# Cutting each weight remainder on GpSimd in four pieces: a two-block fp32 transformer kernel

## The reference

```
for l in range(2):                       # block 1
    h = rms_norm(x, norm_mix_pre[l])
    m = hybrid_mixer(h, w_in[l], ...)    # differential + dilated attention, gates
    x = x + rms_norm(m, norm_mix_post[l])
    h = rms_norm(x, norm_ffn_pre[l])
    g, u = split(h @ w_gate_up[l])       # hidden size 2816
    x = x + rms_norm((silu(g) * u) @ w_down[l], norm_ffn_post[l])
```

## Time and profile before

| | |
|---|---|
| median of three runs | 3269.81 us |
| profiled execution | 3269.45 us |
| its span, first to last instruction | 3267.7 us |
| mean granted TensorE clock | 0.996 of full speed |
| TensorE busy | 3184.0 us (97%) |
| VectorE busy | 1642.2 us (50%) |
| ScalarE busy | 1342.5 us (41%) |
| GpSimd busy | 1378.8 us (42%), 1175.1 of it in L437 |
| DMA | 335.40 MB, mean 103 GB/s |

### The profile page before, as it was taken

How to read it: one execution, slowest core, us unless ns; L and a number is a source line. 1 busy time by engine, 2 the same in 40 slices (tenths; PEclk the granted TensorE clock), 3 DMA queues, 4 the chain that set the end, 5 groups by cost and what they waited for, 6 DMA issues and landing times. The chain is left out here.

```text
span 3267.7 us, 45371 instructions
## 1 busy us (share of the span) xinstructions
PE 3184.0 (97%) x15969; PEld 2535.7 (78%) x15969; DVE 1642.2 (50%) x2602; ACT 1342.5 (41%) x2106; POOL 1378.8 (42%) x696
## 2 busy tenths in 40 slices
PE   8999999999999999999999999999999999999998
PEld 6778887788887778887788886777888867778887
DVE  6853337655627853337655534853333248533332
ACT  6765554322226765553322224454222245532222
POOL 3233334544454223334544454544444535444444
PEclk9999999999999999999999999999999999999999
DMA  3122222255522122222255523202222231122232
GB/s 140 58 81 87 82 86 78 103 188 197 188 102 80 61 78 88 87 87 77 101 201 184 191 94 107 78 31 80 96 96 97 99 116 65 40 84 96 96 103 103
DMA packets 94314, 335.40 MB, mean 103 GB/s; under 512 B 11072, under 2 KB 12288, under 8 KB 93952
## 3 DMA queue, kind: packets, MB, share of 16 engines
q1 hardware_dynamic: 92480, 327.65, 28.9%
q10 hardware_dynamic: 1728, 6.36, 0.5%
HBM read 331.83 MB, written 8.44 MB: 104 GB/s over the span
## 5 line engine op out<-in xcount | busy, mean ns | idle before, releaser
L437 POOL TENSOR_TENSOR wLo<-wring,wHi 128x1024 fp32r<-128x1024 f32 x482 | 1175.1, 2438 | 1709.8 <-ACT wHi L417 1709.4
L461 PE MATMUL psG<-hHi,wHi 128*128 128x512 f32 x2992 | 1185.3, 396 | 12.5 <-DVE ra L1296 4.3
L461 PE MATMUL psG<-hLo,wHi 128*128 128x512 f32 x2992 | 1170.5, 391 | 8.3 <-POOL hLo L486 7.2
L461 PE MATMUL psG<-hHi,wLo 128*128 128x512 f32 x2992 | 1166.0, 390 | 0.0
L417 ACT ACTIVATE wHi<-wring 128x1024 fp32r<-128x1024 f32 x482 | 510.3, 1059 | 970.6 <-PE psG L461 924.0
L461 PEld LDWEIGHTS psG<-hHi,wHi 128*128 128x128 f32 x2992 | 562.6, 188 | 153.6 <-issue 33.1
L461 PEld LDWEIGHTS psG<-hLo,wHi 128*128 128x128 f32 x2992 | 561.8, 188 | 140.1 <-POOL hLo L486 22.1
L461 PEld LDWEIGHTS psG<-hHi,wLo 128*128 128x128 f32 x2992 | 563.0, 188 | 112.9 <-issue 0.5
L461 PE MATMUL psG<-hidHi,wHi 128*128 128x512 f32 x704 | 274.0, 389 | 1.0 <-DVE branch L1453 1.0
L461 PE MATMUL psG<-hidLo,wHi 128*128 128x512 f32 x704 | 273.9, 389 | 0.0
L461 PE MATMUL psG<-hidHi,wLo 128*128 128x512 f32 x704 | 273.9, 389 | 0.0
(11 more groups left out here) (320 smaller groups left out, 3380.0 us busy)
## 6 DMA issues: line engine op xcount, KB each, us to landing
wring<-in_w SPq DMA_DIRECT2D x494, 512.0 KB, 3.2
modw<-in_wmod SPq DMA_DIRECT2D x96, 512.0 KB, 5.4
e_copies<-e_rows ACTq DMA_DIRECT2D x8, 512.0 KB
T_tab<-e_copies SPq DMA_DIRECT2D x4, 1024.0 KB, 5.5
mask<-in_mask SPq DMA_DIRECT2D x2, 1536.0 KB, 5.9
xin_sb<-in_x SPq DMA_DIRECT2D x4, 512.0 KB, 5.1
e_copies<-e_rows ACTq DMA_DIRECT2D x8, 256.0 KB
out<-o_sb SPq DMA_DIRECT2D x4, 512.0 KB, 3.8
```

What stands on the lines that cost most here:

```text
L437: pool.tensor_tensor(wLo[:, c % CUTS, :, :], wring[:, c % RING, :, :], wHi[:, c % CUTS, :, :], ALU.subtract).then_inc(w_cut[c % CUTS], 1)
L461: mm = pe.matmul(psG[:, G.slot(u), :], w[:, c % CUTS, k, :], r(j), start=start and j == 0 and n == 0, stop=stop and j == len(kts) - 1 and ...
```

## The change

Each call of cut_rest issues four subtractions of two channel tiles (256 columns) each in place of one of eight channel tiles (1024 columns). The semaphore is raised once, by the fourth.

```diff
@@ -58,6 +58,7 @@
 CUTS = 2
 MODS = 6 * DM // P
 MW = 1536 + 2 * P
+PIECE = KT // 4
@@ -434,7 +435,10 @@
         def cut_rest(pool, c, i=None):
 
             until(pool, w_high, c + 1 if i is None else i * RING + (c + 1))
-            pool.tensor_tensor(wLo[:, c % CUTS, :, :], wring[:, c % RING, :, :], wHi[:, c % CUTS, :, :], ALU.subtract).then_inc(w_cut[c % CUTS], 1)
+            for k in range(0, KT, PIECE):
+                ins = pool.tensor_tensor(wLo[:, c % CUTS, k:k + PIECE, :], wring[:, c % RING, k:k + PIECE, :], wHi[:, c % CUTS, k:k + PIECE, :],
+                                         ALU.subtract)
+            ins.then_inc(w_cut[c % CUTS], 1)
```

## The result

The changed kernel takes 3340.78 us (median of four runs, 3339.24 to 3342.39) against 3269.87 us for the kernel before, measured beside it. The ratio is 1.0217, with a 95% interval of 1.0205 to 1.0229: 70.9 us slower. The profiled execution took 3342.39 us, its span is 3340.6, 72.9 more than before.

A forecast was written before the change was run, and what follows sets the result against it. TensorE, busy 3184.0 of 3267.7 us, bounds the kernel, so added waits count at once. Terms 63 + 9.5 + 3 + 5.6 - 3 + 0.8 = 79 us on 3269.8 gave 3349, range 3280 to 3362.

The forecast's parts named there:

- all turns taken: Block 1's gate-up: VectorE takes three turns between the pieces of one chunk, 2.84 us more; chance 0.62, range 3325 to 3362.
- the rival that keeps VectorE out: GpSimd runs its four pieces without letting VectorE in; only 0.41 us per chunk counts, 3282 or about 3275; chance 0.17.
- The fixed part: Every GpSimd cut: four pieces take 2.80 us against 2.39 for one instruction, 0.41 more per chunk; bounds zero and 0.53.
- The price of a turn: VectorE getting in between two pieces costs GpSimd 0.45 us for 512 columns, 0.99 for 1024; bounds zero, 0.54 and 1.08.
- Block 1's gate-up: Three VectorE turns in one chunk add 2.84 us against room of 1.36 or 1.44; 44 tiles at 1.44, 63 us.
- The short chunks: Down projections: 28 chunks following a short one have room 0.07 us, each 0.34 over, 9.5 us.
- the leftover products: Four modw products per layer left over at the start of the down projection: 3 us.
- The attention stages: Rope tiles of the first attention and at the second's start: 5.6 us lost in two layers, 3 taken back.
- The room of GpSimd's chunk: Usable slack from GpSimd's end to the chunk's first weight load: 1.36 us in block 1's gate-up, 0.95 next chunk.
- The rival of one product alone: Block 1's gate-up: the second product misses its boundary, a tile costs 0.45 us; 36 us in all, 3306; chance 0.13.
- the faster rival: VectorE's earlier results outweigh GpSimd's later ones: at most 7.8 us of TensorE's waits come back, 3262; chance 0.03.

## Why the prediction was right

The forecast was 3349 us with a range of 3280 to 3362; measured were 3340.8. The forecast's own range, with all turns taken, was 3325 to 3362 and holds it too; the wider one reached down to 3280 only for the rival that keeps VectorE out. The mechanism with its place held: VectorE takes three turns between the four pieces in block 1's gate-up, and the run with the delayed products shows that the turns cost the stretch its time. That the sum of 79 came so near the 70.9 is in part luck: the gate-up was 3 us too dear, the down projections 4 and the branch products 4, and the attention stages 5 too cheap.

*The fixed part.* Taken as 0.41 us per chunk, from back-to-back pairs; an undisturbed cut takes 2.82 us against 2.39, so 0.43. The bound of 0.53, from reported durations, was too high, and the advice to go by the spacing of starts (the Trainium skill, Perfetto Trace Analysis, GPSIMD Engine Instruction) agrees with the trace: a piece reports 0.74 us and starts 0.69 after the last.

*The price of a turn.* Taken as 0.45 and 0.99; the pieces show 0.45 and 0.98. The 0.09 that a turn is cheaper than what VectorE still needs was right.

*Block 1's gate-up.* Taken as 44 x 1.44 = 63 us. Two tiles of the same kind start at 663.31 and 687.85, so two chunks take 12.27 us against 10.88: 1.39. The stretches hold 57.1 us and the last tile of each layer, in the down projection, about 2.8. The 0.05 to 0.09 less have a reason in the rows: after a late chunk the second weight load follows the first after 0.11 us and not 0.23.

*The short chunks.* Taken as 28 x 0.34 = 9.5, with 3 for the leftover products. The four down projections lose 11.1 us, of which 2.8 belong to the gate-up's last tiles, so 8.3. The 3 us for the leftover products do not show in the net: in layer 2 the chunk after the first short one starts 1.0 us later than the pieces alone make it, and in layer 1 the kernel before had itself lost 1.4 us at 887.70, where the load waits for VectorE's copy (L1453), of which 1.0 is gone. Of a wait like that one the prediction said nothing, and a single layer can carry it or not. Here too the first 0.34 is partly given back: after 905.76 the next chunk starts 5.35 us later and not 5.44. In these rows the remainder ends at 905.71 and the load follows at once, as in the earlier trace rows with no room left:

```profile
902.89 2.82 POOL L439 TENSOR_TENSOR wLo<-wring,wHi 128x256 fp32r<-128x256 f32 x4 [2.98 <-ACT wHi L418]
...
905.76 0.19 PEld L465 LDWEIGHTS psG<-hidHi,wHi 128*128 128x128 f32 x1 [0.40 <-POOL wLo L439]
```

*The attention stages.* This term failed in size and in its make-up. I had +5.6 for chunks without room and -3 for VectorE's earlier results, 2.6 in all; the two stages give +7.4. The first attention is a gain (-1.7 in sum: each layer loses 1.7 in its first rope tiles and wins 2.6 after them). The second loses 9.1, or 4.5 a layer. Part of that is the first rope tile there (1.2 a layer, where I had 0.86). Another part is a step that I did not have: VectorE's rotation product (L1295, now L1299) used to start just when GpSimd's cut ended, and now meets the last piece. VectorE, then GpSimd:

```profile
265.35 1.00 DVE L1299 TENSOR_TENSOR tmp<-tmp,ropes 128x512 f32<-128x512 f32 x1 [16.98 <-ACT tmp L1007]
```

```profile
262.98 2.82 POOL L439 TENSOR_TENSOR wLo<-wring,wHi 128x256 fp32r<-128x256 f32 x4 [3.54 <-ACT wHi L418]
```

The cut ends at 265.80; the product needs 1.00 us instead of 0.69, and the instruction behind it (L1300), which frees the PSUM buffer, comes so much later; the chunks of the rope tiles start 0.1 to 0.3 us late. That the one causes the other was read from the trace and not tried. The group's mean went from 692 to 879 ns. The room of GpSimd's chunk says nothing of this: it is a wait in the other direction. The last part, 1.6 us a layer, is TensorE's clock, for which the prediction had no term. After the first rope tile TensorE waits 2.25 us for the remainder, until the load at 196.74, and from 198.0 to 201.4 the granted clock is 0.5 of full speed, the lower of its two levels (1.2 GHz): weight loads start 0.43 us apart there and not 0.23. The same stretch of the changed kernel, and of the run with block 1's gate-up in one piece, whose load comes at 194.26 after the same wait (columns as in the earlier trace rows; the clock is the third number from the end):

```profile
198.00:202.00 4.00, 4.00 (x12) 3.15 (x11) 2.39 (x3) 0.47 (x1) 1.91 (x3) 0.58 0.60 205
```

```profile
195.50:199.50 4.00, 4.00 (x19) 3.27 (x18) 2.38 (x3) 0.50 (x1) 1.94 (x3) 1.00 0.62 201
```

Five runs have the four pieces and the wait of 2.25 us at this place, each in two layers. In five of these ten layers the clock falls behind the wait (both of the changed kernel, layer 2 of the run just named), and in these the second attention takes 353.5 us, in the other five 351.7 to 352.0. In the kernel before, where the wait is 1.01 us, it falls in neither layer. So 3.3 of the 9.1 us are the clock's; what decides whether it falls after a given wait stays open.

*The branch products.* Costed at nothing; they gain 4.3 us. I had read that their cuts have room and did not ask what VectorE wins there, though its 2.37 us per rounding stood on the same list as hidLo.

*The rivals.* VectorE is let in at every boundary in these traces, also when no semaphore stands between the pieces, so the rival that kept it out falls. What the GPSIMD Engine Reference of the Trainium skill says (Instruction dispatch: consecutive instructions are no barrier between the cores) does not keep VectorE out here: hidLo's 1030 ns in the mean against 2323 show it. The rival of one product alone had the right form; its price, 16 us in its own run above the rest, is below the 20 that I had given it. Of the faster rival's 7.8 us, the wait for kLo is gone from TensorE's list, and the one for `ra` is 4.3 us as before.

## What to carry to other kernels

An instruction that holds up another engine also shields its own chain from it: cutting it in pieces lets the other engine in at each boundary, at most of the length of the other's work (0.45 us for a subtraction that takes 0.69 alone, 0.98 for a product that takes 1.23). Before cutting, list what the other engine will have waiting in that time and hold the sum against the room of the chunk; where there is room and the other engine is on the path (the branch products here), the pieces pay, and where there is none, order the other engine's work behind the cut. Also ask what the longer instruction now collides with at its end, not only at its boundaries. And before a wait that lasted longer is given a price, look at the granted clock behind it: here some of the loss was TensorE running at half speed afterwards.

## What the runs showed of the hardware

- Three times in a row a waiting VectorE instruction with two SBUF inputs got in between two GpSimd subtractions that had no semaphore between them (658.74, 659.88 and 661.56). All 88 hidLo subtractions of the changed kernel were let in at the next boundary: each ends 0.55 us after the piece that ran when it was issued. In the cut shown the price to GpSimd was 0.45 us for 512 columns and 0.98 for 1024.
- A VectorE product of 8 columns is held up by GpSimd as a long one is (0.55 us, until the piece's end, in the cut shown), but costs GpSimd nothing that shows.
- The fixed cost of a further GpSimd subtraction is about 0.14 us: 2.39 us for one, 2.54 for two, 2.82 for four and 3.39 for eight pieces of the same 1024 columns.
- After TensorE had waited 2.25 us, its granted clock was 0.5 for 3.4 us in five of ten layers and stayed at 1.00 in the other five, with the same instructions; the drop cost 1.6 us.
